# One exponent for a border tile's context and local scores, and an earlier turn of the next four queries

## What is computed

```python
# A: band of three 128-blocks, sink column, 4 query heads share one key head
s_loc = where(band, q @ k.T * scale, -inf); s_ctx = q @ k_ctx.T * scale
p = softmax(concatenate([s_loc, s_ctx, sink_col]))
# B: neighbourhood on a 16 x 64 grid, relative bias per head
s_loc = where(mask, q @ k.T * scale + bias, -inf); s_ctx = q @ k_ctx.T * scale
p = softmax(concatenate([s_loc, s_ctx]))
o = p_loc @ v + p_ctx @ v_ctx
```

## Time and profile before

| what | value |
|---|---|
| median of 3 runs | 2624.68 us (2622.07 to 2631.15) |
| profiled execution | 2624.9 us, span 2622.9 us |
| mean granted clock of TensorE | 0.966 |
| TensorE matmul busy | 2426.6 us (93%) |
| VectorE busy | 1601.9 us (61%) |
| ScalarE busy | 1033.2 us (39%) |
| GpSimd busy | 268.3 us (10%) |
| DMA, mean over the span | 110 GB/s |

### The profile page before, as it was taken

One profiled execution on the slowest core, in us unless ns is written; L12 is line 12 of the kernel. 1 busy time (PEld: TensorE's weight loads), 2 busy tenths in 40 slices (PEclk: granted clock), 3 DMA queues, 4 the chain that ended last, 5 costly groups with the idle time before them and its releaser, 6 DMA issues. The chain is left out here.

```text
span 2622.9 us, 41034 instructions
## 1 busy us (share of the span) xinstructions
PE 2426.6 (93%) x15675; PEld 2075.1 (79%) x15675; DVE 1601.9 (61%) x2643; ACT 1033.2 (39%) x1983; POOL 268.3 (10%) x249
## 2 busy tenths in 40 slices
PE   5799989888698999999999999998897999999998
PEld 3789877776597788888888799986796888878886
DVE  4623247777557877777678812117348777666677
ACT  2422245555512433323344432134344544444444
POOL 1565300000102000000000200004030000000001
PEclk8899999999889999999999999998898999999999
DMA  8233320000132232322566411100321444377453
GB/s 310 81 114 126 113 55 2 2 1 1 57 129 80 77 104 93 121 94 98 205 202 197 149 61 33 49 29 1 113 89 69 151 159 149 129 266 248 141 181 117
DMA packets 189034, 288.21 MB, mean 110 GB/s; under 512 B 11704, under 2 KB 109948, under 8 KB 188540
## 3 DMA queue, kind: packets, MB, share of 16 engines
q1 hardware_dynamic: 188860, 285.84, 32.7%
HBM read 219.46 MB, written 67.34 MB: 109 GB/s over the span
## 5 line engine op out<-in xcount | busy, mean ns | idle before, releaser
L394 PE MATMUL ps<-w_hi,ht_hi 128*128 128x256 f32 x1744 | 506.0, 290 | 28.6 <-DVE w_lo L379 17.2
L395 PE MATMUL ps<-w_lo,ht_hi 128*128 128x256 f32 x1744 | 499.7, 287 | 0.0
L396 PE MATMUL ps<-w_hi,ht_lo 128*128 128x256 f32 x1744 | 499.5, 286 | 0.0
L394 PEld LDWEIGHTS ps<-w_hi,ht_hi 128*128 128x128 f32 x1744 | 339.4, 195 | 45.5 <-DVE w_lo L379 18.5
L395 PEld LDWEIGHTS ps<-w_lo,ht_hi 128*128 128x128 f32 x1744 | 339.9, 195 | 0.0
L396 PEld LDWEIGHTS ps<-w_hi,ht_lo 128*128 128x128 f32 x1744 | 339.4, 195 | 0.0
L379 DVE TENSOR_TENSOR w_lo<-stage,w_hi 128x2048 fp32r<-128x2048 f32 x31 | 71.4, 2303 | 197.8 <-ACT w_hi L375 197.8
L1665 PE MATMUL ps<-ff_b_hi,ff_a_hi 128*128 128x512 f32 x448 | 174.6, 390 | 2.5 <-DVE ff_b_lo L1653 1.3
L1667 PE MATMUL ps<-ff_b_hi,ff_a_lo 128*128 128x512 f32 x448 | 174.3, 389 | 0.0
L1666 PE MATMUL ps<-ff_b_lo,ff_a_hi 128*128 128x512 f32 x448 | 174.3, 389 | 0.0
L1423 PE MATMUL ps<-ht_hi,swiglu_w_hi 128*128 128x512 f32 x352 | 138.2, 393 | 10.1 <-DVE tmp L1940 7.7
(11 more groups left out here) (356 smaller groups left out, 5538.1 us busy)
## 6 DMA issues: line engine op xcount, KB each, us to landing
ff_a_raw<-ff_act_dram SPq DMA_DIRECT2D x112, 256.0 KB, 2.7
stage<-w_in SPq DMA_DIRECT2D x23, 1024.0 KB, 5.3
swiglu_a_raw<-swiglu_act_dram SPq DMA_DIRECT2D x77, 256.0 KB, 3.2
stage<-w_mod SPq DMA_DIRECT2D x16, 1024.0 KB, 5.5
ff_stage<-w_ff SPq DMA_DIRECT2D x16, 1024.0 KB, 5.5
ff_act_dram<-ff_act_sums SPq DMA_DIRECT2D x16, 1024.0 KB, 4.3
ff_act_dram<-ff_acts SPq DMA_DIRECT2D x16, 768.0 KB, 5.7
swiglu_stage<-w_up SPq DMA_DIRECT2D x11, 1024.0 KB, 5.4
```

The costliest lines, as they stand in the source:

```text
L394: pe.matmul(bank, a, wh[:, k, :], start=(k == 0), stop=False)
L395: pe.matmul(bank, a, wl[:, k, :], start=False, stop=False)
L396: mm = pe.matmul(bank, b, wh[:, k, :], start=False, stop=(k == KT - 1))
```

## The change

`joined` no longer decides how the exponents, the denominators and the wait of the scores are done. A border tile's context scores go through the operation of L921 too, over 256 columns with the zero columns of the inner table, into `masked` beside the local ones, and its minimum starts the second operation over the 512 local columns. One exponent then reads 768 columns of `masked`. The scores of every unit wait for `min_done`. In looped pairs a small memset (L905) stands ahead of a border tile's minimum as well. TensorE's and ScalarE's steps for the next quad move from n % 4 = 1 to n % 4 = 0, VectorE's from n % 4 = 2 to n % 4 = 1.

```diff
--- before.py
+++ after.py
@@ -755,10 +755,8 @@
             if isinstance(u, int) and u == 0:
                 pe.wait_ge(kt_hi, 10)
                 pe.wait_ge(kt_lo, 10)
-            elif joined(*preceding(ph, i, n)[0::2]):
+            else:
                 pe.wait_ge(min_done, 2 * u)
-            else:
-                pe.wait_ge(exp_done, 2 * u)
             if ph == A:
                 parts = [(0, CTX, S, CTX), (1, 0, first * P, width)]
             else:
@@ -810,7 +808,7 @@
                         pe_turn_p(pe, ph, i, n, 0)
                         if behind:
                             pe_values(pe, *behind)
-                        if n % 4 == 1 and next_quad(ph, i, n):
+                        if n % 4 == 0 and next_quad(ph, i, n):
                             pe_turn_q(pe, *next_quad(ph, i, n))
                         pe_turn_p(pe, ph, i, n, 1)
                         if behind:
@@ -843,15 +841,9 @@
             if not isinstance(u, int) or u > 0:
                 act.wait_ge(pt_done, 2 * u - 1 + j)
             low = small[:, j, 2:3]
-            if joined(ph, n):
-                first = 7 if ph == A else 8
-                act.activation(probs_s[:, j, first:8 + CTX + width], masked_s[:, j, first:8 + CTX + width], ACT.Exp, bias=low,
-                               scale=-1.0, accum_out=den[:, n % 2, j, 0:1]).then_inc(exp_done, 1)
-                return
-            act.activation(probs[:, j, 0:CTX], ps[:, 2 * j, 0:CTX], ACT.Exp, bias=low, scale=-1.0,
-                           accum_out=den[:, n % 2, j, 0:1])
-            act.activation(probs[:, j, CTX:CTX + width], masked[:, j, 0:width], ACT.Exp, bias=low, scale=-1.0,
-                           accum_out=den[:, n % 2, j, 1:2]).then_inc(exp_done, 1)
+            first = 7 if ph == A else 8
+            act.activation(probs_s[:, j, first:8 + CTX + width], masked_s[:, j, first:8 + CTX + width], ACT.Exp, bias=low,
+                           scale=-1.0, accum_out=den[:, n % 2, j, 0:1]).then_inc(exp_done, 1)
 
         def turned_p(ph, n):
             cols = P * len(chunks(ph, n))
@@ -898,11 +890,11 @@
                 dve.tensor_copy(masked_s[:, j, 7:8], neg_sink[:, head])
                 dve.drain()
             both = ps[:, 2 * j:2 * j + 2, :].rearrange("p a n -> p (a n)")
+            if ph == B:
+                dve.wait_ge(tab_done, 4 * (i + 1) if joined(ph, n) else 4 * i + 2)
+            if not isinstance(i, int):
+                dve.memset(small[:, j, 5:6], 0.0)
             if joined(ph, n):
-                if ph == B:
-                    dve.wait_ge(tab_done, 4 * (i + 1))
-                if not isinstance(i, int):
-                    dve.memset(small[:, j, 5:6], 0.0)
                 dve.wait_ge(band_in, 16) if ph == A else dve.wait_ge(bias_in, 32)
                 if ph == A:
                     scores, start = both[:, CTX:2 * CTX + width], small[:, j, 3:4]
@@ -912,11 +904,10 @@
                     scores, start, table = both[:, 0:CTX + width], BIG, inner[:, j, :]
                 out = masked[:, j, 0:CTX + width]
             else:
-                dve.wait_ge(tab_done, 4 * i + 2)
-                dve.tensor_reduce(small[:, j, 0:1], ps[:, 2 * j, 0:CTX], AX_X, ALU.min)
+                dve.tensor_tensor_reduce(masked[:, j, 0:CTX], both[:, 0:CTX], inner[:, j, 0:CTX], 1.0, BIG, ALU.add, ALU.min, small[:, j, 0:1])
                 dve.drain()
                 dve.wait_ge(bias_in, 32)
-                scores, start, out = both[:, CTX:CTX + width], small[:, j, 0:1], masked[:, j, 0:width]
+                scores, start, out = both[:, CTX:CTX + width], small[:, j, 0:1], masked[:, j, CTX:CTX + width]
                 table = edge[:, j, at0:at0 + 8, :].rearrange("p a n -> p (a n)")
             dve.tensor_tensor_reduce(out, scores, table, 1.0, start, ALU.add, ALU.min, small[:, j, 2:3]).then_inc(min_done, 1)
 
@@ -934,14 +925,9 @@
             dve.wait_ge(exp_done, 2 * u + 2)
             if not isinstance(u, int) or u > 0:
                 dve.wait_ge(dn_step, u)
-            total = den[:, n % 2, :, 0]
-            if not joined(ph, n):
-                dve.tensor_reduce(dsum[:, :], den[:, n % 2, :, 0:2], AX_X, ALU.add)
-                dve.drain()
-                total = dsum[:, :]
             if not isinstance(u, int) or u > 1:
                 dve.wait_ge(on_evac, u - 1)
-            dve.reciprocal(rden[:, n % 2, :], total).then_inc(dn_step, 1)
+            dve.reciprocal(rden[:, n % 2, :], den[:, n % 2, :, 0]).then_inc(dn_step, 1)
 
         def dve_o(dve, ph, i, n):
             u = unit(ph, i, n)
@@ -989,7 +975,7 @@
                             dve_o(dve, *behind)
                         dve_sums(dve, ph, i, n)
                         dve_p(dve, ph, i, n)
-                        if n % 4 == 2 and next_quad(ph, i, n):
+                        if n % 4 == 1 and next_quad(ph, i, n):
                             dve_q(dve, *next_quad(ph, i, n))
                         if behind:
                             dve_on(dve, *behind)
```

## The result

| what | before | after |
|---|---|---|
| median | 2623.75 us (2622.07 to 2631.15, 4 runs) | 2589.18 us (2583.18 to 2590.21, 4 runs) |
| profiled execution, and its span | 2624.9, 2622.9 us | 2589.41, 2586.8 us |
| mean granted clock | 0.966 | 0.968 |
| first w_out load issued | 699.47 us | 663.63 us |

The ratio of the times is 0.9858, 95% interval 0.9834 to 0.9882. The forecast was 2592 us, range 2585 to 2606; faster by over 0.3% it is. The spans differ by 36.1 us, and a lead of 35.84 us is there when the attention ends.

A forecast was written before the change was run, and what follows sets the result against it. TensorE bounds the attention, so its idle time can be won: 22.6 + 14.0 + 27 x 0.07 = 38.5 us, less 3.9 (tables), 1.0 (late minima) and 1.0 (dearer minima), 32.6 us net, giving 2592 us, range 2585 to 2606.

The forecast's parts named there:

- Part 1: At quad edges, turning the queries one unit sooner removes 15 waits of scores for q_t's split: 22.6 us, 0.07 more each.
- The late minima: VectorE's moved split makes the next minima begin up to 0.3 us late; 0.07 us charged at 15 places, 1.0 us.
- Part 2: One exponent for both halves: scores behind border tiles wait for minima, so 12 waits go, 14.0 us, 0.07 more each.
- Rival (d): Scores behind border tiles wait for the minima instead of the exponent; 14.0 + 0.8 us stay, 2607 us; chance 0.03.
- Minimum of 256 columns at 0.48 us: VectorE's context minimum in border tiles rises from 0.42 to 0.48 us, bounds 0.42 and 0.75; costs 1.0 us.
- Rival (a): VectorE bounds the border units: the 256-column operation costs what 512 columns cost, 8.6 us more, 2601 us; chance 0.12.
- the rule for where it counts: The dearer minimum counts only where VectorE leads, in two units at each of four table places: 1.0 us.
- The tables take back 3.9 us: VectorE's edge tables give gain back as longer o_t waits: 1.0 us at three places, 0.9 where phase A ends.
- The clock, nothing charged: TensorE's granted clock in the attention: the longest new gap, 2.2 us, might lower it, but nothing was charged.
- Rival (b): The clock falls at each table place as gaps grow to 1.6 to 2.2 us: 14 us, 2606 us; chance 0.06.
- (c): The clock falls at a table place and stays low; from the first one on, 155 us more, 2747 us; chance 0.02.
- rival (e): The attention's gain doesn't carry through, as later stages wait for a transfer that starts earlier: no change; chance 0.01.

The follow-up runs named there:

- e2: The changed kernel with the earlier turn of the queries put back to its old units, so the one exponent alone: 2610.75 us, ratio 0.995.
- e1: The kernel before with only the three steps of the queries' turn moved one unit earlier, border tiles as before: 2602.48 us, ratio 0.9917.
- e3: The changed kernel, but scores behind a border tile wait for the exponent (exp_done) again: 2600.13 us, ratio 0.9917.
- e6: The changed kernel with the 256-column minimum operation of border tiles done twice, the first output overwritten: 2596.78 us, ratio 0.9891.
- e7: The changed kernel without the edge and inner tables of pairs 1 to 3 of phase B, which use pair 0's: 2582.5 us, ratio 0.9834.
- e5: The changed kernel itself measured again, nothing edited: 2589.15 us, ratio 0.9864.
- e4: The kernel before with VectorE's split of q_t put ahead of the sums and the copy of prob_t in the same unit: 2607.93 us, ratio 0.9935.
- e12: The changed kernel measured a third time, nothing edited, one run: 2586.49 us.
- e9: The changed kernel with both heads' edge tables built by GpSimd instead of VectorE, started one minimum sooner: 2580.61 us, ratio 0.9833.

## Why the prediction was right, step by step

- **What bounds the stage.** TensorE's idle time did. Its busy time hardly moved (2426.6 to 2424.8 us in the program), and the end came 36 us sooner.
- **Part 1, 22.6 us and 0.07 at each place.** Right. In phase A, turns 0 to 29, seven quads' edges are passed and the gain is 12.66 - 2.30 = 10.36 us, 1.48 us each. The rows of before give 1.40 + 0.07 = 1.47. e2 puts all 15 waits back and e1 takes them away.
- **The start of A, a term the sum did not have.** The prediction read the low clock there only as a price of gaps. It did not see that the turn of the queries, once moved, falls into this stretch, and the stretch became 2 to 3 us shorter.
- **The late minima, 1.0 us.** Not seen. 1.48 us at each edge leaves nothing for them, and no wait of the scores for L912 stands outside of the stage's start. So the 0.3 us was hidden; that the cover named in the prediction, turn and values of TensorE, is what hid it was not tried by itself.
- **Part 2, 14.0 us and 0.07 each.** Right in mechanism and size. e3 puts only the wait back, and 12.8 us of the gain go; its rows give 13.2. Rival (d), scores that wait for the minima instead, falls with the table of waits.
- **Minimum of 256 columns at 0.48 us.** Mis-sized: it takes 0.421, the same as the reduction it replaces (0.422). The slope from 512 to 640 columns did not carry down to 256. It was the lower bound that held, and the term of 1.0 us is nothing. Rival (a), 0.75 us, is out. e6 shows that the rule for where it counts was about right: 5.4 us by the rule, 6.8 measured, of 10.9 added.
- **The tables take back 3.9 us.** Right, and the best-aimed step: o_t waits of 1.6 us at three places and 2.2 at one were forecast, 1.68, 1.54, 1.53 and 2.24 measured. e7 shows that the tables are their cause.
- **The clock, nothing charged.** Nearly right. The fall at the end of A that I named and did not charge came in one of three profiles and cost 1.5 us. Rival (b), a fall at every table place for 14 us, did not happen, nor did (c): within 10 us of the fall the granted clock was 1.00 again.
- **What it carries through, rival (e).** The stage behind starts 35.84 us sooner and the span is 36.1 shorter, so in this pair it carries wholly. In e5 the stage behind starts 37.91 us sooner and the span is 36.0 shorter. What lies behind the attention takes 1918.2 to 1926.3 us in the profiles here, so the carrying is shown only within that scatter.
- **The sum.** 32.6 us forecast, 35.1 clean. The difference of 2.5 us is the dearer minima (1.0) and the late minima (1.0), both charged and not paid, and 0.5 us which I cannot place. With the start of A the attention gained 37 to 38 us, some 5 more than the sum. The medians show only 34.6 us. In the first profile a fall cost 1.5 us and the scores of unit 1 started 0.65 us later than before, which leaves 35.84 us where the attention ends; what remains is scatter between executions. So the mechanism was right, but that the median came within 2.8 us of the forecast is in part luck, since a missing gain and these losses nearly cancel.

## What to carry to other kernels

A wait of the bounding engine is worth its recorded idle time plus the overlap that it breaks (0.07 us here), if the next thing late is found too: 38.5 us of waits gave 35.1 mostly because 3.9 us of them turned into another wait, which the rows of the table places told beforehand. Look first at what stands ahead of the late instruction in its own queue: swapping it with a copy in the same unit gave 16.3 of the 19.2 us that the move to another unit gave, the start of A apart. Look too at where a moved step lands: here it shortened the start of A by 2 to 3 us, which nobody had counted. And where PSUM is what is waited for, a cheap operation that already reads it (the minimum) can write the copy to SBUF in the same pass, at the price of the reduction it replaces, and release the bank one engine earlier.

## What the runs showed of the hardware that I had not expected

- **Width against time of the minimum's operation.** 0.421 us for 256 columns, 0.751 for 512, 0.882 for 640, 1.022 for 832. The forms over 256 and 832 columns start from an immediate, the others from a value in SBUF, and the two kinds lie on different lines: between the former 1.04 ns a column, which puts 512 columns at 0.69 us. That the kind of start is what costs the 0.06 us was not tried.
- **Falls of the granted clock are not a function of the gap.** The same kernel with the same 2.23 to 2.24 us wait fell in one execution of three; over all kernels here whose wait at the end of A was 2.09 us or more, it fell in five of eight (the changed kernel's first profile, e1, e3, e4, e6, but not e5, e7, e12); the exponent-only kernel fell twice behind 1.67 us in one execution and never behind it in the next. A fall cost 0.7 to 2.7 us and the clock came back. In none of them did the clock fall at every gap of B, so the rule of the Trainium skill that the prediction weighed (TensorE: Matmul & The Clock Gate, A second HAM failure mode: psum-queue depth-cycling) has no case of standing oscillation in the attention here, only single falls.
- **GpSimd beside VectorE.** An operation of VectorE with both inputs in SBUF went from 1.08 us to between 1.25 and 1.67 us, longer by 0.17 to 0.59 us for 0.30 to 0.72 us of overlap. Operations with an input in PSUM kept their lengths, though one of them started late (e9). GpSimd takes 1.92 to 1.97 us for the 896-column table that VectorE does in 1.08.
